# Two transformer blocks on one core: the second block's mixer with its norms applied after the transposes and the projections

## What is computed

```python
hn = rms_norm(x, norm_mix)
proj = hn @ w_in                      # 1024 x 2336
qa, ka, va, cq, ckv, kr, hc, bc, cc = split(proj)   # 384 384 384 256 128 32 256 256 256
qa, ka = rms_norm(qa, q_norm_a), rms_norm(ka, k_norm_a)       # per head of 64
out_a = neighbourhood_attention(qa, ka, va, rpb)    # 6 heads
qb = rms_norm(cq, cq_norm) @ w_uq                   # 256 x 576
kv = rms_norm(ckv, ckv_norm) @ w_ukv                # 128 x 768
out_b = mla_attention(norm+rope(qb), norm+rope(kv_nope, kr), v)   # 6 heads of 96
out_c = bc * conv3(cc * hc, conv_w)
o = concat(rms_norm(out_a), rms_norm(out_b), rms_norm(out_c)) # 384 + 384 + 256, gain out_norm
x = x + o @ w_out
h = rms_norm(x, norm_ffn)
aff = softmax(h @ w_router + b_router)              # 16 experts
gate, idx = top_k(aff.T, 32)                        # 32 tokens per expert
x = x + scatter(gate * ((silu(h[idx] @ w_gate) * (h[idx] @ w_up)) @ w_down))
```

## Time and profile before

| what | us |
|---|---|
| median of 3 runs (2189.39 to 2192.83) | 2190.3 |
| the profiled execution, its own time | 2190.9 |
| its span | 2188.8 |
| busy: TensorE (matmul) | 1728.2 (79%) |
| busy: TensorE weight loads | 956.5 (44%) |
| busy: VectorE | 560.9 (26%) |
| busy: ScalarE | 283.1 (13%) |
| busy: GpSimd | 103.4 (5%) |
| HBM read, mean | 273 GB/s |

### The profile page before, as it was taken

How to read it: one execution, slowest core, us unless ns; L and a number is a source line. 1 busy time by engine, 2 the same in 40 slices (tenths; PEclk the granted TensorE clock), 3 DMA queues, 4 the chain that set the end, 5 groups by cost and what they waited for, 6 DMA issues and landing times. The chain is left out here.

```text
span 2188.8 us, 19513 instructions
## 1 busy us (share of the span) xinstructions
PE 1728.2 (79%) x8196; PEld 956.5 (44%) x8196; DVE 560.9 (26%) x1187; ACT 283.1 (13%) x738; POOL 103.4 (5%) x143
## 2 busy tenths in 40 slices
PE   6999999999999999888756575665988756575655
PEld 3566888444778864456412121211455412121211
DVE  2654566222624210263201010101173200010101
ACT  1142000012510000124100000000133100000000
POOL 0011000000200000230000000000130000000000
PEclk8999999999999999889788787878989778787878
DMA  9961887546136422731399999999631499999997
GB/s 375 332 209 36 264 306 281 195 146 210 42 105 218 150 93 77 229 154 77 156 424 425 424 425 424 424 425 415 215 154 77 190 424 425 424 426 424 424 425 308
DMA packets 181967, 599.50 MB, mean 274 GB/s; under 512 B 18576, under 2 KB 71440, under 8 KB 132624
## 3 DMA queue, kind: packets, MB, share of 16 engines
q1 hardware_dynamic: 181662, 598.08, 70.2%
q10 hardware_dynamic: 242, 0.53, 0.1%
HBM read 594.80 MB, written 3.80 MB: 273 GB/s over the span
## 5 line engine op out<-in xcount | busy, mean ns | idle before, releaser
L1053 PE MATMUL ps<-ring,wide 128*32 128x512 f32 x2304 | 359.6, 784 | 240.7 <-DMA ring<-in_w_up 104.4
L826 PE MATMUL ps<-hT,ring 128*128 128x256 f32 (+1 forms) x1664 | 311.7, 349 | 0.0
L1053 PEld LDWEIGHTS ps<-ring,wide 128*32 128x32 f32 x2304 | 86.4, 138 | 502.1 <-issue 234.2
L826 PEld LDWEIGHTS ps<-hT,ring 128*128 128x128 f32 x1664 | 278.6, 192 | 35.0 <-issue 4.9
L582 PE MATMUL ps<-ring,hT 128*128 128x512 f32 (+1 forms) x448 | 184.0, 571 | 3.9 <-DVE hT L1470 2.0
L703 PE MATMUL ps<-ring,hT 128*128 128x512 f32 (+1 forms) x448 | 178.5, 555 | 2.7 <-ACT hT L1139 2.7
L1053 PE MATMUL ps<-extra,wide 128*32 128x512 f32 x768 | 121.2, 789 | 74.7 <-DMA extra<-in_w_up 34.4
L855 PE MATMUL ps<-ring,wide 128*128 128x512 f32 x352 | 157.5, 609 | 7.9 <-DVE wide L1771 7.9
L2027 DVE TENSOR_TENSOR wide<-ps,wide 128x512 f32<-128x512 f32 x16 | 10.3, 686 | 522.3 <-PE ps L1053 522.3
L582 PEld LDWEIGHTS ps<-ring,hT 128*128 128x128 f32 x448 | 85.4, 192 | 99.2 <-issue 90.3
L703 PEld LDWEIGHTS ps<-ring,hT 128*128 128x128 f32 x448 | 81.2, 194 | 93.8 <-issue 93.8
(11 more groups left out here) (224 smaller groups left out, 1310.7 us busy)
## 6 DMA issues: line engine op xcount, KB each, us to landing
ring<-in_w_gate SPq DMA_DIRECT2D x24, 4096.0 KB, 33.6
ring<-in_w_up SPq DMA_DIRECT2D x24, 4096.0 KB, 30.5
ring<-in_w_down SPq DMA_DIRECT2D x24, 4096.0 KB, 34.1
ring<-in_w_mod SPq DMA_DIRECT2D x24, 2048.0 KB, 13.3
ring<-in_w_up SPq DMA_DIRECT2D x44, 1024.0 KB, 7.9
ring<-in_w_in SPq DMA_DIRECT2D x18, 2048.0 KB, 14.0
extra<-in_w_gate SPq DMA_DIRECT2D x8, 4096.0 KB, 33.1
extra<-in_w_up SPq DMA_DIRECT2D x8, 4096.0 KB, 35.7
```

What stands on the lines that cost most here:

```text
L826: last = mm(ps[2 * (j % 2) + half][:, f * T + o:f * T + o + n], wt[:, k, w:w + P], h8[:, k, o:o + n], start=k == 0, stop=k == KD - 1)
L1053: last = mm(ps[bank + n][e * CAP:(e + 1) * CAP, :], lhs[:, k, e * CAP:(e + 1) * CAP], wt[:, e, k % PAIR, n * N:(n + 1) * N], start=k == 0, ...
```

## The change

In words, part by part:

- **Stream.** TensorE transposes x itself (`flip_raw`), by chunk: chunk 0 of layer 0 ahead of the last part of the down projection, chunk 0 of layer 1 as soon as its two scatter additions are done. ScalarE evacuates four of the eight blocks of a chunk, VectorE the other four, with norm_mix (in layer 0 the product of it and the final gain, `gmix`) as the scale. The roots, `rmix`, are applied when the projections are read out of PSUM. In layer 0 x is scaled by the final norm in place, beside the projection. The mean is one VectorE operation, the root one GpSimd operation (two in layer 0).
- **Tiles.** w_in is cut into tiles of 416 (cq, ckv, kr), 512, 512, 512 (in two pieces) and 384 columns and used in this order; the columns in `proj2` are laid out anew. The first two tiles are projected chunk 0 and 0, then 1 and 1, with the flip of chunk 1 between.
- **Latents.** They are made of the compressed parts without their roots, which come in when the latents are read out of PSUM. All squares of the heads move from VectorE to ScalarE. GpSimd's mask of the bias stands ahead of the compressed root. The flips of q and k stand inside the last tile.
- **Output.** The row blocks 0, 1, 2, 6, 7 of the output (NEAR) are scaled, flipped within the last map and multiplied first; blocks 3, 4, 5 (FAR, the second kind of attention) are flipped without their root and summed apart, and the root is applied in the addition to x.
- **Router.** It goes by chunk: raw x is flipped, the router's weights are the stationary side, 32 columns wide in four column groups, a product with `fold` adds the four up, the root comes in with the bias.
- **Experts.** Normed x is written in contiguous blocks by ScalarE (`xk`); TensorE waits for ScalarE's part of the gathered rows only at tile 4; the four scatter products have a PSUM bank each.

The core of the diff:

```diff
-IN2_ORDER = (2, 3, 0, 1, 4)
-B2_TILES = [("in", i) for i in IN2_ORDER[0:4]] + [("small", 0), ("in", IN2_ORDER[4]), ("out", 0), ("out", 1)]
+IN2_TILES = ((CQ2, ((1152, 416),)), (0, ((0, 512),)), (512, ((512, 512),)), (1024, ((1024, 128), (1568, 384))),
+             (1536, ((1952, 384),)))
+B2_TILES = [("in", i) for i in range(5)] + [("small", 0), ("out", 0), ("out", 1)]
...
+            def flip_raw(L, c):
+                pe.wait_ge(*x_ready(L, c, 1))
+                for hf in range(2):
+                    for q in range(4):
+                        k = 4 * hf + q
+                        last = nc.tensor.transpose(ps[4 + 2 * c + hf][:, q * P:(q + 1) * P], x[:, c, k * P:(k + 1) * P], ident)
+                    last.then_inc(mix[L].up("b2_x_flipped"), 1)
...
-                        if (c, n) == (1, 1) and L == 0:
-                            flip_stream(2, 0)
+                        if (c, n) == (1, 1):
+                            flip_stream(2, 0) if L == 0 else flip_raw(0, 0)
...
+                raw_ready(0)
+                project(0, 0)
+                flip_raw(L, 1)
+                project(1, 0)
+                raw_ready(1)
+                project(0, 1)
+                project(1, 1)
...
+                project(2, 0)
...
+                        last.then_inc(s.up("b2_latent_done"), 1)
+                project(2, 1)
...
+                project(3, 0)
+                project(3, 1)
+                project(4, 0)
+                pe.wait_ge(*s.at("b2_latent_by_act", 4))
+                pe.wait_ge(*s.at("b2_latent_by_dve", 4))
+                pe.wait_ge(*s.at("b2_heads_normed", 2))
...
+                project(4, 1)
+                pe.wait_ge(*s.at("b2_block_ready", 5))
...
+                out2(4, NEAR, 0, 0).then_inc(s.up("b2_out_done"), 1)
+                pe.wait_ge(*s.at("att_out_read", MAPS2))
...
+                out2(5, NEAR, 0, 1).then_inc(s.up("b2_out_done"), 1)
+                out2(0, NEAR, 1, 0).then_inc(s.up("b2_out_done"), 1)
+                out2(1, NEAR, 1, 1).then_inc(s.up("b2_out_done"), 1)
...
+                out2(2, FAR, 0, 0).then_inc(s.up("b2_out_done"), 1)
+                out2(3, FAR, 0, 1).then_inc(s.up("b2_out_done"), 1)
+                out2(6, FAR, 1, 0).then_inc(tile_done, 1)
...
+                    for k in range(KD):
+                        o, w = 32 * (k % 4), (L * KD + k) * EXP
+                        last = mm(ps[2][o:o + 32, c * P:(c + 1) * P], router[:, w:w + 32], h8[:, k, c * P:(c + 1) * P],
+                                  start=k < 4, stop=k >= 4)
...
+                flip_rows(0)
+                out2(7, FAR, 1, 1).then_inc(tile_done, 1)
...
+                route(0)
+                flip_rows(1)
+                logits(0)
+                route(1)
+                pe.wait_ge(*s.at("b2_logits_ready", 1))
+                logits(1)
...
                 pool.wait_ge(*s.at("b2_bias_loaded", 16 * 16))
...
+                pool.wait_ge(*s.at("b2_compressed_sumsq", 1))
+                inv_root(s, 4, "invC", "eps6", "b2_compressed_rstd", ssc, rsc)
...
+                latent_norm(0, qb, 0, t768[:, 0:384])
+                latent_mean(1, squares[:, 384:1536])
+                project_read(3)
+                latent_norm(0, qb, 1, t768[:, 0:384])
+                latent_norm(1, kb, 0, t768[:, 0:384])
+                project_read(4)
+                latent_norm(1, kb, 1, t768[:, 0:384])
...
+                    stt(xv, ps[2 + 4 * c + n][:, :], rsm[1][:, 3 * c + 2:3 * c + 3], xv, ALU.mult, ALU.add)\
+                        .then_inc(s.up("b2_mixer_added"), 1)
```

More of the change, by code:

```diff
@@ L183, in at @@
         per = self.counts[name]
+        if name in SHARED_COUNT:
+            return self.sems[name], sum(per[:self.turn + self.block]) + k
         return self.sems[name], (sum(per[:self.turn]) if isinstance(per, tuple) else self.turn * per) + k
@@ L197, in end @@
             per = self.counts[name]
-            if n != (per[self.turn] if isinstance(per, tuple) else per):
+            at_ = self.turn + self.block if name in SHARED_COUNT else self.turn
+            if n != (per[at_] if isinstance(per, tuple) else per):
                 MISCOUNT.append((name, self.turn, n, per))
@@ new lines, in _ @@
+                project(2, 1)
+                pe.wait_ge(*s.at("b2_latent_by_act", 2))
+                pe.wait_ge(*s.at("b2_latent_by_dve", 2))
+                for c in range(2):
+                    for hf in range(2):
+                        last = mm(ps[4 + 2 * hf + c][:, 0:384], cT[:, 2, c * P:(c + 1) * P],
+                                  ukv[:, hf * 384:(hf + 1) * 384], start=True, stop=True)
+                        last.then_inc(s.up("b2_latent_done"), 1)
+                project(3, 0)
@@ new lines, in _ @@
+                for c in range(2):
+                    dve.wait_ge(*s.at("b2_head_squared", c + 1))
+                    v = ss[:, 12 * c:12 * c + 12]
+                    nc.vector.tensor_reduce(v, squares[:, 768 * c:768 * (c + 1)].rearrange("p (h d) -> p h d", h=12),
+                                            AX.X, ALU.add).then_inc(s.up(), 1)
+                    dve.wait_ge(*s.own())
+                    ts(v, v, 1.0 / HD, 1e-6, ALU.mult, ALU.add).then_inc(s.up("b2_head_mean"), 1)
+                latent_mean(0, kN[:, :, :].rearrange("p b t -> p (b t)"))
```

905 lines of the change are left out of this document (526 added, 379 removed), and 8 rows, old and new, of tables (B1_COUNT, B2_COUNT).

## The result

The changed kernel takes 2124.3 us (2121.2 to 2126.0), a ratio of 0.9695 to the kernel before (95% interval 0.9678 to 0.9712). The forecast was 2137 in a range from 2130 to 2155. The profiled execution has a span of 2123.8 us against 2188.8.

A forecast was written before the change was run, and what follows sets the result against it. The engines' chain through mixer and router, passed twice, was taken as the bound, with expert stages bound by DMA. Gains of 16.6, 11.8, 1.2, then 10.7, 11.8, 1.2, and 0.4 made 53.7 us off 2190.9: 2137, range 2130 to 2155.

The forecast's parts named there:

- the second line of the table: Stretch from mask 0 to the gather; the forecast summed a gain of 11.8 us in each layer.
- the third: Stretch from the gather to the issue of pair 4; the forecast summed a gain of 1.2 us per layer.
- the first: Stretch from end of down (layer 0) or first scatter product (layer 1) to mask 0; gains summed 16.6 and 10.7 us.
- the fourth: Expert stage, from issue of pair 4 to first scatter product or last addition; gains summed 0 and 0.4 us.
- part 1: Mixer front, up to the first projection: gain 12.6 us in layer 0 and 6.2 us in layer 1.
- part 2: Projection to scores: 73.4 us with no wait; masking the bias ahead of the compressed root costs 0.
- part 3: VectorE's last key norm, before mask 0: takes 6.7 us beside GpSimd's taps, with ends 2.8 and 9.0.
- part 4: Attention's twelve maps: nothing removed, cost 0, up to 1.1 us either way per layer.
- part 5: Output projection after the last map: multiplying starts earlier, in two sums; gain 6.3 us.
- part 6: Router: 2.2 us for a chunk's 16 records; gain with output projection 11.8 us per layer, ends 9 and 13.
- part 7: Experts' first group and end: earlier start gains 1.2 us per layer, the end 0.4, loads zero.
- Rivals (a) to (d): Joints cost, 2152, 0.17; one half fails, 2161, 0.08; compressed root behind bias, 2195, 0.03; DMA bounds mixer, does nothing, 0.02.

## Why the prediction was wrong

The path was right: the time came off the chain through mixer and router, and the expert stage stayed DMA's. What failed are the costs of three steps, numbers 5 to 7 below. Of the 12.7 us between 2137 and 2124.3 the second line of the table gives 7.0, the third 7.3 and the first 1.9, the fourth takes 5.9 back; 1.05 are the earlier end of the first block, 1.4 the distance of the profiled execution from the median. That the forecast missed by no more is in part luck, since the growth of the expert stage hid 5.9 us of what the other two gave.

1. **Front, layer 0 and 1 (part 1), and projection to scores (part 2): right.** Projection started at 873.34, and the first block had ended 1.05 us earlier in this execution, so 874.4 on the old clock (said 875.5). The scores came 72.8 us later (said 73.4). In layer 1 projection at 1496.89, 5.8 us behind the first scatter product (said 1533.7 against 1527.52, 6.2). The compressed root came at 913.6 (said 915.9), and undoing the order changed nothing.
2. **The last norm beside the taps (part 3): right.** 6.6 us, 947.04 to 953.68, said 6.7; without the taps it is 2.8, the lower end. The upper end, 9.0, for which I had taken the rule of the Trainium skill (SBUF — State Buffer, on port sharing) strictly, was a misreading: the page has the pair of ports held for one whole instruction, not for a queue of them. The trace agrees with that, since the held steps end 0.1 to 0.6 us after a tap, and with the page's rule for one input in SBUF, since the mask keeps its 0.68 us. That the norm could stand ahead of the last read, for 14.5 us, I had not seen.
3. **Attention (part 4): right within its bound** for the changed kernel (the last map's products end 35.4 us behind mask 0, before 34.75).
4. **Output product (part 5): right.** From the last map's end to the end of the product, the first flip of x in it, 29.8 us, said 30.7.
5. **Router (part 6): the first step that failed.** "I take 2.2" for the 16 records of a chunk; they take 0.65, less than a third, and both chunks' records stand in the chain. From the end of the product to the top-k's copy it was 6.7 us, said 10.1: 3.4 per layer. My rows were of 512 moving columns; the records here have 128. The full-width form at the same clock took 1.85, so the four groups side by side give 2.9 times. My upper bound came from a row at the low clock: the old product's 6.98 us ran at a granted clock of 0.50. The Trainium skill (TensorEngine Tiling (Array Packing), on theoretical speedup) has up to 4x for four such tiles, and the trace agrees with 2.9x. The 1.7 us for both chunks that I worked out from it were a quarter of the 6.98; at the full clock a quarter of the full-width 3.78 is 0.9, and measured are 1.3.
6. **First group (part 7): the second step.** I took the gather and the first pair as unchanged. The gather became 2.0 and 1.7 us shorter, since `xk` is contiguous: I had named the write of it and not its reader. The first pair became 1.7 us shorter, since the wait that goes had cost the clock; I had counted the wait's 1.2 us alone. Together 3.7 us in layer 0 and 3.4 in layer 1.
7. **The expert stage (part 7): the third step, on the other side.** I wrote "so the expert stage is DMA's and stays 449 us whatever the engines do". It is DMA's, but its length hung on the place of a tensor that the change moved: the pairs into `extra` lost the 0.24 us by which they had been ahead of the others, and the stages 5.5 us together.

Of the range: the lower bound of the router was 1.8 us a chunk, and gather, first pair and expert stage had no bounds at all. Rivals (a) to (d) didn't come about.

## What to carry to other kernels

- When data get a new layout, cost every reader of it as well as its writer; here the reader's weight loads gave 3.7 us over both layers, and the writer's longer passes cost nothing, since nothing waited for them.
- A product with a narrow stationary operand in column groups should be costed from the number of columns that move through it (128 here, not the 512 of my rows), and a wait by the clock that it leaves behind as well as by its length.
- When a stage is bound by DMA, compare its length in two profiles before and after any edit that adds a column to a table: tensors that are allocated later move.

## What the hardware showed that was not expected

- The transfers to one tensor of SBUF are faster or slower by its place: a pair of 4 MB lands 9.71 us after the one before it where the tensor lies 84 bytes past a multiple of 512, and 9.94 with 244 or 0, as in the ring. With 11 such pairs a stage of layer 1 takes 448.8 to 449.1 us in the one case and 451.3 to 451.5 in the other.
- A float32 weight load of 128 by 128 with a stride of 8 takes 0.336 us at 1.2 and 2.4 GHz alike, a contiguous one 0.333 and 0.192.
- A VectorE step with two inputs in SBUF is held by a GpSimd instruction with two inputs there and slips in between two of them (the smallest step takes 1.31 us instead of 0.25), one with an input in PSUM isn't (0.68).
- The same idle time of 1.2 us lowered the clock in the kernel before, in both layers and both profiles, and not in two variants of the changed one.
